# Both expert layers of a two-block transformer: matmuls by pairs of channel groups, wide ones first, narrow ones behind

## The reference

```
q = (hc @ w_query) ...                       # 8 heads
s1, s2 = scores against 128 + 128 sub-keys; top 16 of each; top 16 of their 256 sums
u = jnp.take(expert_u, eidx, axis=0)
a = jnp.einsum('thkd,td->thk', u, hc)
act = jax.nn.gelu(a) * g
vv = jnp.take(expert_v, eidx, axis=0)
return jnp.einsum('thk,thkd->td', act, vv)
```

## Time and profile before

| | us |
|---|---|
| median of 3 runs | 1343.51 |
| lowest and highest run | 1341.03, 1345.34 |
| span of the profiled execution | 1339.8 |
| TensorE busy | 1311.4 |
| VectorE busy | 1008.9 |
| ScalarE busy | 823.8 |

### The profile page before, as it was taken

The page is one execution under the profiler, slowest core; times in us unless marked ns, Lnnn a source line. Parts: engine busy times, 40 slices in busy tenths (PEclk is TensorE's granted clock), DMA queues, the critical chain, the costliest instruction groups (busy, mean ns, idle before and its releaser), DMA issues.

```text
span 1339.8 us, 24822 instructions
## 1 busy us (share of the span) xinstructions
PE 1311.4 (98%) x9818; PEld 1259.1 (94%) x9818; DVE 1008.9 (75%) x1849; ACT 823.8 (61%) x1679; POOL 504.0 (38%) x248
## 2 busy tenths in 40 slices
PE   9999899999999999999999999999998999999997
PEld 8999799999999999999989999999998999999997
DVE  3573545759999888899978798998768846888843
ACT  6563556545455888888755565555656666666552
POOL 3745457678901000000024444334103453763442
PEclk9999999999999999999999999999999999999999
DMA  8433345555656555545579999999863544555552
GB/s 304 136 114 114 111 131 184 162 173 176 201 187 206 192 162 170 170 161 169 164 254 324 358 344 331 335 336 329 266 211 118 162 138 143 173 169 177 173 189 95
DMA packets 74299, 268.36 MB, mean 200 GB/s; under 512 B 8252, under 2 KB 8636, under 8 KB 74184
## 3 DMA queue, kind: packets, MB, share of 16 engines
q1 hardware_dynamic: 64968, 233.22, 53.3%
q0 software_dynamic: 9216, 33.56, 6.9%
HBM read 265.70 MB, written 1.05 MB: 199 GB/s over the span
## 4 chain that ended last, share of the span: by engine, by line
PE 80%; DVE 13%; ACT 4%; DMA 1%; issue 1%; POOL 0%; SPq 0%; DVEq 0%; ACTq 0%
PE PS L601 79%; DVE SPL L1516 2%; ACT SPL L1078 2%; DMA RAW<-in_ev 1%; DVE ub L2215 1%; DVE ixu L1806 1%; DVE Ssc L1800 1%; DVE ixu L1797 1%; DVE ub L2211 1%; DMA RAW<-in_dense 1%; DVE ub L2208 0%; DVE bias L1595 0%; DVE top L1803 0%; DVE top L1794 0%; DVE HF L1533 0%
## 5 line engine op out<-in xcount | busy, mean ns | idle before, releaser
L1078 ACT ACTIVATE SPL<-RAW 128x1024 fp32r<-128x1024 f32 x432 | 456.1, 1058 | 347.3 <-PE PS L601 328.8
L601 PE MATMUL PS<-HS,SPL 128*128 128x224 f32 (+2 forms) x4016 | 542.5, 293 | 7.5 <-DVE SPL L1516 4.7
L601 PEld LDWEIGHTS PS<-HS,SPL 128*128 128x128 f32 x4016 | 510.7, 190 | 21.6 <-DVE SPL L1516 7.8
L2238 POOL TENSOR_TENSOR SPL<-RAW,SPL 128x1024 fp32r<-128x1024 f32 x148 | 359.5, 2433 | 349.1 <-ACT SPL L1078 348.9
L1516 DVE TENSOR_TENSOR SPL<-RAW,SPL 128x1024 fp32r<-128x1024 f32 x284 | 354.1, 1249 | 158.9 <-ACT SPL L1078 157.3
L601 PE MATMUL PS<-asp,SPL 128*128 128x448 f32 (+1 forms) x2048 | 322.1, 320 | 1.7 <-DVE GB L1916 1.2
L601 PEld LDWEIGHTS PS<-asp,SPL 128*128 128x128 f32 x2048 | 305.6, 189 | 17.8 <-DVE GB L1916 1.7
L2268 POOL DMA_INDIRECT rows<-in_er,RS x16 | 27.9, 1745 | 283.7 <-PE PS L601 250.1
L601 PE MATMUL PS<-HXb,SPL 128*128 128x256 f32 x720 | 90.0, 284 | 1.6 <-DVE SPL L1516 1.1
L601 PEld LDWEIGHTS PS<-HXb,SPL 128*128 128x128 f32 x720 | 87.5, 188 | 2.8 <-DVE SPL L1516 2.0
L1291 ACT ACTIVATE oh<-oh,T3f 128x128 f32<-128x128 f32 x224 | 71.4, 404 | 0.0
(11 more groups left out here) (286 smaller groups left out, 1457.3 us busy)
## 6 DMA issues: line engine op xcount, KB each, us to landing
RAW<-in_dense SPq DMA_DIRECT2D x176, 512.0 KB, 3.5
RAW<-in_eu SPq DMA_DIRECT2D x128, 512.0 KB, 3.6
RAW<-in_ev SPq DMA_DIRECT2D x128, 512.0 KB, 5.9
bias<-in_nab SPq DMA_DIRECT2D x2, 768.0 KB, 8.4
XT<-in_xT SPq DMA_DIRECT2D x4, 256.0 KB, 6.7
out_y<-HF SPq DMA_DIRECT2D x4, 256.0 KB, 2.2
c<-in_c SPq DMA_DIRECT2D x1, 960.0 KB, 8.6
c<-in_c SPq DMA_DIRECT2D x1, 512.0 KB, 4.7
```

Source lines behind the costliest of these rows:

```text
L601: return e.matmul(out, l, r, start=start, stop=stop, skip_group_check=skip)
L1078: e.activation(spl(n)[0], raw(n), ACT.Copy).then_inc(*up("act_high", ("hi", n)))
L2238: e.tensor_tensor(lo, raw(n), hi.bitcast(f32), ALU.subtract).then_inc(*up("pool_low", ("lo", n)))
```

## The change

In both places the loop over single groups becomes one over pairs. Where a group's wide matmul was followed by its narrow one, the two wide matmuls of a pair come first and the two narrow ones behind them. The same matmuls run on the same operands; only the order inside a pair differs. The slots 0 to 47 keep their order. Where a bank is waited for in step 0 of the second layer, the second bank of a pair is now waited for ahead of the first narrow matmul, and the hand-over of both banks of a pair comes with its narrow matmuls.

```diff
-                    for c in range(8):
-                        w.wait_ge(*at("hlo", 1, c))
-                        if i < ROUTED:
+                    if i < ROUTED:
+                        for c in range(8):
+                            w.wait_ge(*at("hlo", 1, c))
                             t = mm3(ps[:, 0:W], (hi[:, c, :], lo[:, c, :]), (HS[:, 0, c, 0:W], HS[:, 1, c, 0:W]), c == 0, c == 7)
-                        else:
-                            mm(ps.rearrange("p (s t) -> p s t", s=2)[:, :, 0:W], hi[:, c, :], HS[:, :, c, 0:W], c == 0, False, True)
-                            t = mm(ps[:, 0:W], lo[:, c, :], HS[:, 0, c, 0:W], False, c == 7, True)
+                    else:
+                        for c0 in range(0, 8, 2):
+                            for c in (c0, c0 + 1):
+                                mm(ps.rearrange("p (s t) -> p s t", s=2)[:, :, 0:W], hi[:, c, :], HS[:, :, c, 0:W], c == 0, False, True)
+                            for c in (c0, c0 + 1):
+                                t = mm(ps[:, 0:W], lo[:, c, :], HS[:, 0, c, 0:W], False, c == 7, True)
...
-                    for c in (0, 1, 4, 5, 7, 6, 2, 3) if i == 0 else range(8):
-                        o = bank(VB[c])
-                        if i == 0:
-                            w.wait_ge(*(at("ev", *used[VB[c]]) if VB[c] != 7 else at("std", 1)))
+                    for pair in ((0, 1), (4, 5), (7, 6), (2, 3)) if i == 0 else ((0, 1), (2, 3), (4, 5), (6, 7)):
                         for v, (hi, lo) in zip(vs, parts_v):
                             s = asp[v % 4]
-                            mm(o.rearrange("p (s t) -> p s t", s=2)[:, :, 0:W], hi[:, c, :],
-                               s.rearrange("p (s t) -> p s t", s=2)[:, :, 0:W], v == 0, False, True)
-                            t = mm(o[:, 0:W], lo[:, c, :], s[:, 0:W], False, v == NE - 1, True)
+                            for c in pair:
+                                o = bank(VB[c])
+                                if i == 0:
+                                    w.wait_ge(*(at("ev", *used[VB[c]]) if VB[c] != 7 else at("std", 1)))
+                                mm(o.rearrange("p (s t) -> p s t", s=2)[:, :, 0:W], hi[:, c, :],
+                                   s.rearrange("p (s t) -> p s t", s=2)[:, :, 0:W], v == 0, False, True)
+                            for c in pair:
+                                t = mm(bank(VB[c])[:, 0:W], lo[:, c, :], s[:, 0:W], False, v == NE - 1, True)
```

More of the change, by code:

```diff
@@ L915, in pe_program @@
                             mm(bank(VB[c])[:, W:256], yrow[:, c * 128:c * 128 + 128], con("fold"), False, False, True)
-                    for c in (0, 1, 4, 5, 7, 6, 2, 3) if i == 0 else range(8):
-                        o = bank(VB[c])
-                        if i == 0:
-                            w.wait_ge(*(at("ev", *used[VB[c]]) if VB[c] != 7 else at("std", 1)))
+                    for pair in ((0, 1), (4, 5), (7, 6), (2, 3)) if i == 0 else ((0, 1), (2, 3), (4, 5), (6, 7)):
                         for v, (hi, lo) in zip(vs, parts_v):
                             s = asp[v % 4]
-                            mm(o.rearrange("p (s t) -> p s t", s=2)[:, :, 0:W], hi[:, c, :],
-                               s.rearrange("p (s t) -> p s t", s=2)[:, :, 0:W], v == 0, False, True)
-                            t = mm(o[:, 0:W], lo[:, c, :], s[:, 0:W], False, v == NE - 1, True)
-                        if i == NE - 1:
-                            t.then_inc(*up("pe_expert", ("vsum", c), *[("used", cur[0]), ("used", cur[0] - 1), ("v", i)] * (c == 7)))
+                            for c in pair:
[6 more added lines that the diff above has]
+                                t = mm(bank(VB[c])[:, 0:W], lo[:, c, :], s[:, 0:W], False, v == NE - 1, True)
+                                if v == NE - 1:
+                                    t.then_inc(*up("pe_expert", ("vsum", c), *[("used", cur[0]), ("used", cur[0] - 1), ("v", i)] * (c == 7)))
                     if i < NE - 1:
```

## The result

Over 20 runs each, the changed kernel takes 1344.87 us (median; 1343.15 to 1348.20) and the kernel before 1342.26. The ratio is 1.0024, 95% interval 1.0018 to 1.0030: by it 3.2 us more (2.4 to 4.0). I had forecast 1335.5, which was 8 us less than the 1343.5 of three runs that I started from.

What follows compares the result with a forecast made beforehand. TensorE's matmul spacing was taken to bound both layers: 9.7 us saved, less 0.7, 0.2 and 0.8 given back, leaves 8.0; 1343.5 - 8.0 = 1335.5 us. Range for 8 in 10: 1330 to 1344 us.

Steps and rivals of the forecast that it cites:

- What bounds the stage: Both layers: TensorE is busy 98% of the span and hardly waits, so the spacing of matmuls sets the time.
- rules 1 and 2: TensorE: loads start at least 0.11 us apart, and none before the matmul in front of its own begins.
- a wide matmul of 0.190 us: Both layers: price taken for a wide matmul, under which the next load hides; two groups fall from 0.627 to 0.615 us.
- 0.123 for the exposed load: Narrow to next matmul, waiting for a load that starts with the narrow one: 0.123 us, paid once in four, not twice.
- the weak term: The wide matmul's price, taken as 0.190 us; at 0.196 the total saving would be 4.5 us instead of 9.7.
- The rival of no change: Both layers: each matmul has its own price in any order, wide 0.201 us; time stays 1343.5 us; chance 0.17.
- rule 2: TensorE: a load can't start before the matmul in front of its own begins; one set of weights can wait.
- The rival of a dearer wide matmul: Both layers: a wide matmul behind a wide one costs 0.215 us; 11 us slower, 1354.6 us; chance 0.08.
- What is given back: Losses against the gain: 0.7 us to ScalarE's weighing, 0.2 to VectorE's GB product, 0.8 to late transfers around 744 to 800 us.
- The end of the second layer: Bank hand-overs shift, but TensorE's 3.48 us wait there doesn't hang on the order within the step: nothing lost.
- theory C: Added during the experiments: a ready wide matmul costs 0.2066 us, one waiting for its load behind a narrow one 0.107.

Runs made afterwards that it cites:

- e5: Steps 1 to 96 of the second layer replaced by twelve matmul patterns of other widths and mixes, base kernel not named; 512 columns took 0.233 us.
- e9: Steps 1 to 96 of the second layer replaced by twelve patterns with smaller loads or other operand places, base kernel not named; 256 columns took 0.117 us.
- e12: Changed kernel with the asp tiles 16 bytes lower, gap between their parts kept; second-layer steps of 2.507 us, no total given.
- e14: Kernel before, in its old order, with the asp tiles 16 bytes lower; ratio 1.0020, steps of 2.533 us.
- e7: Order by groups of four with one small extra matmul ending every eighth second-layer step, its load width varied; steps of 2.507 or 2.533 us, no total given.
- e15: Order by groups of four with the asp tiles 16 bytes lower; one run, 1348.10 us, steps of 2.547 us from step 3 on.
- e2: Kernel before with the pair order in the second layer alone; ratio 1.0031, 1344.85 us, steps of 2.533 us.
- e3: Changed kernel with groups of four in both layers, four wide matmuls then four narrow ones; ratio 1.0026 to the kernel before, 1344.95 us.
- e6: Changed kernel with groups of eight in both layers, eight wide matmuls then eight narrow ones; ratio 1.0045 to the kernel before, 1347.06 us.

## Why the prediction was wrong

**What bounds the stage, and which loads start when: right.** TensorE's spacing sets both layers, and loads start as the rules 1 and 2 say, in the new order too.

**The step that failed: a wide matmul of 0.190 us, and with it 0.123 for the exposed load.** I called it the weak term. From a difference of row starts (0.10 us for a narrow matmul) I had 0.19 to 0.20, and I took 0.190 because it left 0.12 to 0.13 from load to stream at two places. Both remainders were reckoned with that 0.19 itself, so they could not confirm it: with 0.202 they are 0.11 and 0.12. Wide matmuls alone take 0.202 with a load of 32 columns and 0.203 to 0.207 with a full one, narrow ones alone 0.100 and 0.112, and 0.202 + 0.111 meets the old pair's 0.313. Then a load that could only start with the narrow matmul costs no more than one that follows another at its distance, and there is nothing to be saved by paying the one instead of the other: 0.615 was forecast for two groups, and the patterns have 0.6267 to 0.6333. The Trainium skill's formula that I set beside the value, 189 ns for 448 columns ("TensorE: Matmul & The Clock Gate", Back-to-back issue gap), is given there for an isolated matmul. It is not what this kernel's matmuls take one behind another: by it 512 columns are 216 ns, and e5 has 233.

**The rival of no change** named this ("0.201 in its own right") and the row that spoke for it, the spacing of 0.120 for 256-column matmuls. I argued it away with rule 2. e9 shows 256 columns at 0.117 with a load of a quarter of the columns, where rule 2 has nothing to push back: it was the matmul's own price. I had given the rival 0.17.

**The rival of a dearer wide matmul** had the right sign and the wrong mechanism. Its 0.215 is a row's length from start to start, and no wide matmul alone takes more than 0.207. The loss of 26 ns a step, 3.3 us, goes with the order and the operand's address together (e12 to e14). Why a place suits one order and not the other wasn't found. The order by fours also depends on phase alone, so a rule of address alone can't be it.

**What is given back:** there was no gain to give back. The first layer lost 0.8 us. What was lost near 764 us varied from nothing (e7, e15) to 6.1 us (e2, with its drop of the clock) and shows no relation to the order. The end of the second layer was right for pairs, and e3 and e6 show from where it costs.

**Left open:** whether the remaining 5 ns between 0.202 and 0.207 are paid by the wide matmul or by the next load (theory C put them on the wide one and had 0.632 for the pair order, against 0.6333 from asp and 0.6267 to 0.6300 from HS), and why 16 bytes of address change the step. No run found a version that beats the kernel before: the fastest step, 2.500, would be worth 0.9 us and costs 2.3 us at the layer's end.

## What to carry to other kernels

When the gain rests on how a measured sum splits into two terms, measure one of them alone before believing in it; a second place that shows the same sum doesn't confirm the split. A reordering on an engine that is always busy is worth only what an exposed wait costs over the engine's own price, and the own price comes from a stream of equal instructions. Effects of 1% on such a stream can belong to an operand's address: move a buffer by 16 bytes before blaming the order.

## What the runs showed of the hardware that I had not expected

- Matmuls on split f32 operands, each with its load, were spaced at 0.45 to 0.46 ns a column from 256 columns up: 512 columns 0.233 us, 448 from 0.202 to 0.207, 384 0.173, 320 0.147, 256 0.117, at a granted clock of 1.00. Below that the full load sets 0.112 (224 and 128 columns alike; 224 with a load of 32 columns take 0.100). On the unsplit f32 operand HF the kernel before has matmuls of 256 columns at 0.216.
- The same repeated sequence of matmuls can run at two speeds (2.507 and 2.533 us for 16, by fours; 2.500 and 2.540, by eights) and keep either for dozens of steps. By fours, one small matmul more switched it four times; in e3 and e6 the change came at a delay, of 0.1 us and a wait of 1.0.
- All step lengths seen, 2.500, 2.507, 2.520, 2.533, 2.540 and 2.547 us, lie on a grid of 6.7 ns.
- Waits and the granted clock near 764 us and behind the layers made differences of 1 to 6 us between single profiled executions, as large as the effect sought; step lengths repeated within 2 ns.
- 16 bytes in the base of the moving operand turned 2.507 into 2.533 for one order and the reverse for another.
